# Modulations 3 to 5 in feed-forward groups 1 to 3, the mix norm's first tile in the last group, three buffers in the decay block

## The reference

```
mods = (silu(c) @ w_ada + b_ada)                     # 9 vectors of 1024 for each of 9 sequences
sh1, sc1, gt1, sh2, sc2, gt2, sh3, sc3, gt3 = mods
x = x + 0.5 * gt1 * swiglu(rms_norm(x, g1) * (1 + sc1) + sh1)      # first feed-forward
P = (rms_norm(x, g2) * (1 + sc2) + sh2) @ w_in                      # input projection, 2560 columns
#   columns 0..1791 -> RWKV-7 heads, 1792..2559 -> sliding-window attention
#   decay d = exp(-exp(w_log)), w_log and a from two 64-wide products; keys normed; running products of d
x = x + gt2 * concat(rwkv7(P), attention(P)) @ w_out
x = x + 0.5 * gt3 * swiglu(rms_norm(x, g3) * (1 + sc3) + sh3)      # second feed-forward
y = rms_norm(x, g_final)
```

## Time and profile before

| | |
|---|---|
| median of 3 runs | 2608.36 us (2606.34 to 2609.14) |
| profiled execution, its own time | 2612.36 us |
| its span | 2610.6 us |
| PE busy | 2461.0 us, 94% of the span, 22194 matmuls |
| DVE / ACT / POOL busy | 1134.9 / 389.7 / 495.5 us |
| mean granted TensorE clock | 0.96 |

### The profile page before, as it was taken

How to read it: one execution, slowest core, us unless ns; L and a number is a source line. 1 busy time by engine, 2 the same in 40 slices (tenths; PEclk the granted TensorE clock), 3 DMA queues, 4 the chain that set the end, 5 groups by cost and what they waited for, 6 DMA issues and landing times. The chain is left out here.

```text
span 2610.6 us, 51884 instructions
## 1 busy us (share of the span) xinstructions
PE 2461.0 (94%) x22194; PEld 2331.8 (89%) x22194; DVE 1134.9 (43%) x2521; ACT 389.7 (15%) x894; POOL 495.5 (19%) x233
## 2 busy tenths in 40 slices
PE   5999999999999699998689999988999999999996
PEld 4999999999998598886279996888999999999995
DVE  4533344434441554343566654217444344433335
ACT  4100000000000324343511113113000000000003
POOL 3322122112210221110500004314221222122110
PEclk8999999999999799998699999898999999999997
DMA  8211111111113331011510001212101111111102
GB/s 319 81 49 32 48 48 30 34 48 48 48 32 129 102 99 37 25 33 47 203 46 4 4 4 61 80 30 81 49 18 47 48 48 48 48 48 42 38 0 76
DMA packets 157638, 151.14 MB, mean 58 GB/s; under 512 B 21441, under 2 KB 138866, under 8 KB 156969
## 3 DMA queue, kind: packets, MB, share of 16 engines
q1 hardware_dynamic: 156824, 142.29, 17.3%
q0 software_dynamic: 528, 4.53, 0.4%
q10 hardware_dynamic: 144, 2.23, 0.2%
HBM read 137.98 MB, written 11.34 MB: 57 GB/s over the span
## 5 line engine op out<-in xcount | busy, mean ns | idle before, releaser
L474 PE MATMUL bank<-hh,f_up_hi 128*128 128x364 f32 (+1 forms) x2112 | 697.0, 330 | 11.8 <-ACT hh L414 9.4
L475 PE MATMUL bank<-hl,f_up_hi 128*128 128x364 f32 (+1 forms) x2112 | 696.0, 330 | 0.0
L476 PE MATMUL bank<-hh,f_up_lo 128*128 128x364 f32 (+1 forms) x2112 | 695.7, 329 | 0.0
L474 PEld LDWEIGHTS bank<-hh,f_up_hi 128*128 128x128 f32 x2112 | 398.8, 189 | 14.8 <-issue 14.8
L872 DVE TENSOR_TENSOR f_prod<-f_silu,bank 128x364 f32<-128x364 f32 x132 | 70.2, 532 | 780.9 <-PE bank L476 780.9
L475 PEld LDWEIGHTS bank<-hl,f_up_hi 128*128 128x128 f32 x2112 | 398.8, 189 | 0.0
L476 PEld LDWEIGHTS bank<-hh,f_up_lo 128*128 128x128 f32 x2112 | 398.8, 189 | 0.0
L489 DVE SCALAR_TENSOR_TENSOR x<-bank,mods,x 128x364 f32<-128x364 f32 (+2 forms) x552 | 310.7, 572 | 200.4 <-PE bank L476 185.1
L725 POOL TENSOR_TENSOR f_up_lo<-f_up_raw,f_up_hi 128x2048 fp32r<-128x2048 f32 x44 | 202.9, 4610 | 803.1 <-DVE f_up_hi L859 803.1
L474 PE MATMUL bank<-f_a_hi,f_dn_hi 128*128 128x364 f32 (+1 forms) x1056 | 347.0, 329 | 0.6 <-issue 0.6
L476 PE MATMUL bank<-f_a_hi,f_dn_lo 128*128 128x364 f32 (+1 forms) x1056 | 346.9, 328 | 0.0
(11 more groups left out here) (348 smaller groups left out, 2855.4 us busy)
## 6 DMA issues: line engine op xcount, KB each, us to landing
f_up_raw<-in_ffn_w_gu SPq DMA_DIRECT2D x88, 512.0 KB, 4.9
f_dn_raw<-in_ffn_w_down SPq DMA_DIRECT2D x22, 1024.0 KB, 7.7
gates<-in_w_ada SPq DMA_DIRECT2D x16, 1024.0 KB, 4.8
ada<-in_w_ada SPq DMA_DIRECT2D x12, 1024.0 KB, 15.9
late<-in_w_ada SPq DMA_DIRECT2D x8, 1024.0 KB, 5.2
w_in_raw<-in_w_in SPq DMA_DIRECT2D x16, 512.0 KB
x_spill<-x POOLq DMA_DIRECT2D x1, 4352.0 KB, 15.1
x_in<-in_x_prompt SPq DMA_DIRECT2D x8, 512.0 KB, 8.3
```

The lines of the kernel that those rows point to most:

```text
L474: pe.matmul(out, wh, rh, start=(n == 0), stop=False)
L475: pe.matmul(out, wh, rl, start=False, stop=False)
L476: ins = pe.matmul(out, wl, rh, start=False, stop=(n == last))
```

## The change

Three parts. (1) Modulations 3, 4 and 5 are made in feed-forward groups 1, 2 and 3, one in each group, which become a loop of their own; the four loads of a modulation go one after another through the raw buffer of the down weights, which stands empty then. Modulation 4 is finished (`finish_mods`) at the start of the last group's down sums. (2) The last group no longer holds modulation products. It holds the loads of the first two `w_in` chunks, the split of the first, the write of x to DRAM tile by tile (now SP's queue), means of the mix norm for tiles 0 and 1, and the whole scaling of tile 0, whose 8 steps on DVE stand one behind each down sum of the third tile. The projection block begins with the split of chunk 1 and tiles 1 and 2 of the norm; PE starts with product (0,0). Chunk 0 of `w_in` has a third pair of split buffers. (3) The decay block makes only modulations 6 to 8; its small weights and the first modulation load are issued at the end of the projection block; three buffers take the place of two.

```diff
...
 
+    def step(self, dve, t, c):
+        k, (a, n), v = self.k, self.spans(t), KD * t + c
+        if c == 0:
+            dve.wait_ge(self.spread_mm, t + 1)
+        if v >= 4:
+            if c % 2:
+                dve.wait_ge(self.lo_odd, (v - 3) // 2)
+            else:
+                dve.drain()
+        dve.scalar_tensor_tensor(self.t[c % 4][:, 0:n], k.x[:, c, a:a + n], k.mod(self.i_shift + 1, c),
+                                 self.bank[t][:, 0:n], ALU.mult, ALU.mult).then_inc(self.t_done, 1)
+        if c % 2 == 1 and c >= 3:
+            self.low(dve, t, c - 3, self.lo_even)
+        if c == KD - 1:
+            self.low(dve, t, KD - 2, self.lo_even)
...
     if first:
-        ada = Ada(k, "ada", (0, 1, 2), [HH_AT + 8 * KB * s for s in range(8)] + [WT_AT + KB * a for a in (24, 32, 40, 48)], 7, [(7, 256)])
-        late = Ada(k, "late", (3, 4), [WT_AT, WT_AT + 40 * KB], 7, [(7, 256), (0, 0)])
+        ada = Ada(k, "ada", [HH_AT + 8 * KB * s for s in range(8)] + [WT_AT + KB * a for a in (24, 32, 40, 48)], 7)
+        late = Ada(k, "late", [WT_AT + 40 * KB], 7)
...
+        mix = k.mix = Norm(k, "mix", 3, 0, WT_AT + 8 * KB, WT_AT + 20 * KB, WT_AT + 28 * KB)
+        x_final, k.spilled = k.sem("x_final"), k.sem("x_spilled")
+    LATE = range(1, 4) if first else range(1, 1)
...
+            if first:
+                with sp.Fori(LATE.start, LATE.stop) as g:
+                    next_up(g, 0)
+                    sp.wait_ge(dn_lo_done, g + 1)
+                    for q in range(4):
+                        if q == 3:
+                            next_up(g, 1)
+                        if q:
+                            sp.wait_ge(late.used, 4 * g + q)
+                        late.load(sp, g + 2, q, 0)
+                    sp.wait_ge(late.used, 4 * g + 4)
+                    load_dn(g + 1)
...
             if first:
                 sp.wait_ge(up_lo_done, FC * NGRP)
-                sp.wait_ge(dn_lo_done, NGRP)
-                for s in range(8):
-                    late.load(sp, s)
+                win.load(sp, 0, win.first[0])
+                win.load(sp, 1, win.first[1])
+                for t, (a, n) in enumerate(TILES):
+                    sp.wait_ge(x_final, 2 * t + 2)
+                    sp.dma_start(k.dram["x_spill"][:, :, a:a + n], k.x[:, :, a:a + n]).then_inc(k.spilled, 16)
...
+            if first:
+                win.low(pool, 0)
+                mix.odd_lows(pool, 0)
...
                     pe.wait_ge(up_lo_done, FC * g + j + 1)
                     for t in range(NT):
+                        u = NT * j + t
                         up(g, j, t)
-                pe.wait_ge(dn_lo_done, g + 1)
-                for t in range(NT):
-                    down(g, t)
+                        if modulation and 1 <= u <= 4:
+                            if u == 1:
+                                pe.wait_ge(dn_free, ND * g + 4)
+                            late.product(pe, u - 1, 0, 4 * g + u - 4)
+                if modulation:
+                    late.turn(pe, g - 1, late_turned)
+                downs(g)
+                if modulation:
+                    pe.wait_ge(late.added, g)
 
             def first_group():
...
-                        if u in (0, 1, 4, 5):
-                            s = {0: 0, 1: 2, 4: 4, 5: 6}[u]
-                            late.product(pe, s)
-                            late.product(pe, s + 1)
-                        if u == 3:
-                            late.turn(pe, 0)
                 pe.wait_ge(dn_lo_done, g + 1)
-                pe.wait_ge(late.rows, 2)
                 for t in range(NT):
-                    down(g, t)
-                    if t == 0:
-                        late.turn(pe, 1)
+                    for c in range(KD):
+                        down(g, t, c)
+                        if t >= 1 and c == 3:
+                            mix.means(pe, t - 1)
+                        if t == 1 and c == KD - 1:
+                            mix.spread(pe, 0)
 
...
+            if first:
+                with pe.Fori(LATE.start, LATE.stop) as g:
+                    group(g, True)
+            with pe.Fori(LATE.stop, NGRP - (1 if first else 0)) as g:
...
+            if first:
+                for j in range(2):
+                    mix.squares(act, 0, j, x_final)
+                mix.roots(act, 0)
+                for j in range(2):
+                    mix.squares(act, 1, j, x_final)
+                mix.highs(act, 0, True)
 
...
 
-            def group(g):
+            def group(g, modulation=False):
                 for u in range(NU):
                     gated(g, u)
                     if u % NT == NT - 1:
                         j = u // NT
                         up_head(j, FC * g + FC + j + 1, NU * g + NT * (j + 1))
+                    if modulation and u == 4:
+                        late.copy(dve, g)
+                if modulation:
+                    late.add(dve, g - 1, g + 2, late_turned)
                 for v in range(ND):
...
-                        late.add(dve, 0)
-                    if first and u == 5:
-                        late.copy(dve, 1)
+                if not first:
+                    for v in range(ND):
+                        summed(g, v)
+                    return
+                dve.wait_ge(dn_lo_done, NGRP)
+                win.high(dve, 0)
+                finish_mods(dve, k, 4)
                 for v in range(ND):
+                    t, c = v // KD, v % KD
                     summed(g, v)
-                    if first and v == KD:
-                        late.add(dve, 1)
+                    if c in (3, KD - 1):
+                        dve.drain().then_inc(x_final, 1)
+                    if t == 1 and c == 6:
+                        mix.inverse(dve, 0)
+                    if t == 2:
+                        mix.step(dve, 0, c)
+                mix.inverse(dve, 1)
 
...
+class InWeights:
...
+        self.first = [k.at(f"w_in_first{j}", WT_AT + 4 * KB * j, [P, KD, P]) for j in range(2)]
+        self.raw = [k.at(f"w_in_raw{j}", R2_AT + 4 * KB * j, [P, KD, P]) for j in range(2)]
+        hi = [k.at(f"w_in_hi{j}", at, [P, KD, P], F32R) for j, at in enumerate((GATE_AT, GATE_AT + 8 * KB, WT_AT + 40 * KB))]
+        lo = [k.at(f"w_in_lo{j}", at, [P, KD, P], F32R) for j, at in enumerate((GATE_AT + 4 * KB, GATE_AT + 12 * KB, WT_AT + 44 * KB))]
...
+            win.load(sp, 3, win.raw[1])
             norm.ready(sp, NT - 1)
-            sp.wait_ge(spilled, 16)
+            sp.wait_ge(k.spilled, 16 * NT)
+            sp.wait_ge(lo_done, 2)
             sp.dma_start(cos[:], d["cos"]).then_inc(tab_in, 16)
...
+            sp.wait_ge(lo_done, NC)
+            sp.dma_start(k.w2a2[0:HD, :], d["rwkv_w2"][0]).then_inc(k.lora_in, 16)
+            sp.dma_start(k.w2a2[HD:P, :], d["rwkv_a2"][0]).then_inc(k.lora_in, 16)
+            sp.dma_start(k.keep[:], d["scan_keep"]).then_inc(k.keep_in, 16)
+            sp.wait_ge(mm_done, at(NC - 2, NT - 1))
+            k.gates.load(sp, 6, 0, 0)
...
 
             for t in range(NT):
                 norm.ready(pe, t)
+                if t == 1:
+                    norm.spread(pe, 2)
                 for n in range(2):
                     if t == 0:
                         pe.wait_ge(lo_done, n + 1)
                     product(n, t)
+                    if t == 0 and n == 0:
+                        norm.spread(pe, 1)
+                        norm.means(pe, 2)
                 if t == 0:
-                    norm.spread(pe, 2)
+                    previous()
             for n in range(2, NC):
                 pe.wait_ge(lo_done, n + 1)
...
-            for s in range(16):
-                ada.load(sp, s)
+            for s in range(1, 12):
+                if s >= 3:
+                    sp.wait_ge(ada.used, s - 2)
+                ada.load(sp, 6 + s // 4, s % 4, s % 3)
             sp.wait_ge(k.shift_out, 32)
...
                 if 1 <= i < PAIRS:
                     back(i)
-                if i in (4, 8, 11):
-                    for q in range(4):
-                        ada.product(pe, 4 * (4, 8, 11).index(i) + q)
-                if i in (5, 9):
-                    ada.turn(pe, (i - 5) // 4)
+                if i == 5:
+                    ada.turn(pe, 0, turned)
+                if i in (4, 8):
+                    modulation(i // 4 - 1)
+            ada.turn(pe, 1, turned)
+            modulation(2)
             pe.wait_ge(rates_done, 2 * NU)
             pe.wait_ge(rk_done, 1)
             for i in range(NU):
                 bonus(i)
-                if i == 1:
-                    ada.turn(pe, 2)
                 if i == 5:
-                    for s in range(12, 16):
-                        ada.product(pe, s)
-                if i == 9:
-                    ada.turn(pe, 3)
+                    ada.turn(pe, 2, turned)
...
+            def modulation(n):
+                ada.add(dve, n, 6 + n, turned)
+                if n:
```

(6 more changed lines are left out.)

318 lines of the change are left out of this document (159 added, 159 removed).

## The result

| | before | changed | ratio, 95% interval |
|---|---|---|---|
| first comparison, 4 runs each | 2608.1 us | 2582.7 us (2581.2 to 2587.3) | 0.9906 [0.9889, 0.9924] |
| a second, later, 7 and 4 runs | 2609.9 us | 2580.8 us (2579.0 to 2583.3) | 0.9888 [0.9872, 0.9905] |

The account below looks back on a forecast made before the run. PE was taken as the bound, so time counts only where it waits, runs at low clock or loses work. Gains of 4.1 + 16.7 + 14.0 = 34.8 us gave 2577.6 profiled, 2573.5 for the median; range 2562 to 2586.

Parts of the forecast that it names:

- a pair took 1.93 us, one is 0.97 ... and I allow 0.5: Feed-forward groups 1 to 3: four added modulation products cost 3.9 us plus 0.5 for turns, 4.4 a group, 13.2 in all.
- DVE's tail: End of the last group: DVE's third-tile sums and norm steps end about 16.6 us after PE starts that tile's down sums.
- Both reasons go: Projection block's start: DVE's 16.11 us wait for w_in goes, since loads are issued a group earlier and the spill is split.
- product (0,0) 4.0, plus 2.0 ...; spread 0.8; then tile 1's scaling: Projection block's start: first product, low-clock extra and spread precede DVE's 8.4 us scaling, within 35.2 us to the third weight.
- The wait of 3.08 for w2a goes: Decay block's start: PE's 3.08 us wait for w2a vanishes, so everything up to lora 4 is 3.1 us earlier.
- the forecast's middle: Middle of the decay block: products 4 to 7 end about 1267, third tile's sigmoids begin about 1271.3 instead of 1275.71.
- The term behind the first bonus, 4.6: Decay block's end: first bonus to next block takes 5.0 to 5.5 us instead of 10.4, a gain of 4.6.
- the fourth is issued only after product 8 has run: Third modulation of the decay block: fourth load issued at 1278.7, first bonus at 1285.3 against 1294.68, 9.4 us gained.
- (a): Rival: exclusive DVE/POOL port lock in the last group's tail and beside tile 1 holds DVE 3.9 us and more; 2579; chance 0.14.
- (b): Rival: ACT, DVE and POOL, not loads, pace the decay block's middle; 7 us less gain, 2580.5; chance 0.12.
- (c): Rival: in groups 1 to 3 the single buffer makes twelve products wait 7 us and more, above 2650; chance 0.03.
- (d): Rival: the gap only moves, PE's wait for the norm appears in full in the last group; 2585 to 2590; chance 0.04.

Follow-up runs that it names:

- the second profiles: Repeat profiles of the unchanged kernel before (2610.4 us) and of the changed kernel with nothing altered (median 2580.8 us).
- the norm's own experiment: Changed kernel with the mix norm wholly in the projection block again, early input-weight loads and spill by tiles kept: 2584.2 us, ratio 0.9896.

## Why the prediction was right, and where not

**Direction and shape were right, the size was read too large**: every stretch gained where it was said to. The median came out at 2582.7 us where 2573.5 was forecast. That is inside the stated range but above the forecast's own 2566 to 2581: the range holds because it was widened for the rivals and the bounds of the parts. Of the 9.2 us missed, 4.0 are the difference between profile and median that was carried over unchanged (the changed kernel's profile lies at its median), 6.3 are the three parts together, and 1.2 the other way were gained outside them, where nothing was forecast. Of the marks it set, it met: PE without a wait in groups 1 to 3, the first product 17 us after the first third-tile sum (862.72 to 879.45: 16.7), first bonus at 59 us (59.4), waits for gates 6 to 8 us (7.7), decay block under 85 (82.3). Missed by little: groups of 76.2 us (76.9), PE standing 6 to 7 us at the end of the last group (8.25), the last group at 82 to 84 us (84.8 with that stand). Not met: PE's waits at tile 1 and at the third tile, forecast as 2 to 3 and 2 us, both for DVE; they were 3.63, released by POOL's low part, and 0.60.

**Part 1, forecast 4.1, measured 2.3.** The step that failed is "a pair took 1.93 us, one is 0.97 ... and I allow 0.5". The pair's second half ran behind a product, the new ones stand alone between up units, and each costs 1.20 with its two seams; 4.4 us a group were reckoned. Taking them out gave 15.0 us back, 5.0 a group. That the loads are hidden held.

**Part 2, forecast 16.7, measured 13.3.** Reckoned from S (861.7): first product at S + 17.8 against 17.4, behind it 37.2 against 35.2, and 1.1 more ahead of S. The terms of DVE's tail were near: a sum with its step 1.40 us where 1.52 was reckoned. Behind the start the terms were, as measured and as reckoned: first product 6.5 and 6.0, spread of tile 1 until DVE starts 1.1 and 0.8, tile 1's scaling with its tail 9.2 and 9.3, spread and third tile 12.3 and 11.1, two products 8.1 and 8.0. The step mis-sized most is the spread of the third tile: PE had stood 3.6 us from 892.6, its clock was low again until 901.8, and DVE's start came 2.09 us after this spread's, where it was 1.14 for tile 1. No term held that. The slow products beside it cost nothing, since PE still waits 0.60 for DVE behind them. Near in its terms, the part was wrong in its account. "Both reasons go" is true of the weights' wait: with the early loads and the spill by tiles, without the early norm, the gain is 12.6. But the norm ahead of the block, on which most of my arithmetic went, gave 0.6 or nothing, because the step "product (0,0) 4.0, plus 2.0 ...; spread 0.8; then tile 1's scaling" was taken over as it stood in the code and not asked whether it need be so. In it DVE, the engine I had named as late next, waits 7.2 us for a spread queued behind a product that nobody needs yet. Moving it, with the sums and the spread of tile 2, gave 6.7.

**Part 3, forecast 14.0, measured 12.9** (and 13.0 between the second profiles, 90.5 and 77.5). "The wait of 3.08 for w2a goes" was mis-sized: it is 1.6 to 1.8 in two other profiles. And the forecast's middle, in which PE's products pace the block, is refuted: with the loads gone waits for ACT take their place (4.1 to 13.0 us). The term behind the first bonus, 4.6, does not follow from its own row: 10.4 less 5.0 to 5.5 is 4.9 to 5.4. It measured 4.1, and 6.5 between the second profiles. What saved the number is that the forecast itself took lora 5 to 7 out of PE's hands (it named ACT and DVE, the traces show ACT and POOL), and that the term that counts was put right: "the fourth is issued only after product 8 has run".

**The rivals.** (a) The port lock in full did not come. In the last group DVE's lows and POOL's subtracts alternate and never meet. Behind it they do; DVE's and POOL's timelines there:

```profile
893.35 0.95 POOL L407 TENSOR_TENSOR hl<-mix_t,hh 128x364 fp32r<-128x364 f32 x1 [1.53 <-ACT mix_t L417]
893.77 1.44 DVE L399 SCALAR_TENSOR_TENSOR hl<-mix_t,mods,hh 128x364 fp32r<-128x364 f32 x2
901.71 0.82 POOL L407 TENSOR_TENSOR hl<-mix_t,hh 128x296 fp32r<-128x296 f32 x1 [0.23 <-ACT mix_t L417]
901.96 0.90 DVE L399 SCALAR_TENSOR_TENSOR hl<-mix_t,mods,hh 128x296 fp32r<-128x296 f32 x1
```

Two lows take 1.44 us where two alone took 1.10, one takes 0.90 where another took 0.52: 0.7 us in all. Twice DVE's low starts first and POOL's subtract is the longer one, 1.33 us at 889.38 and 1.07 at 900.41 where it takes 0.95 and 0.82. That is the direction of the rule that the prediction cites from the Trainium skill (SBUF — State Buffer, "SBUF: two separate sides"), at less than the price of the rival, since the two engines seldom met. (b) is true of the middle, as the experiments without loads and with two buffers show, but its price of 7 us did not come: the gains ahead of the middle and behind it stayed. (c) did not come; landings in the single buffer were 4.8 to 5.8 us. (d) forecast 2585 to 2590 for a gap that only moves. Its time did not come, but its thought, that the early norm buys nothing and the end of the wait for the loads all, is nearer to what the norm's own experiment showed than my account was.

## What to carry to other kernels

Ask of each moved piece what it is worth alone, with the other pieces in place: gains measured one at a time need not add, since two edits may cure the same wait or both hold a third piece (here the spill by tiles), and the larger gain may lie with the smaller edit. When the forecast names the engine that is late next, look through the queues of the engines that feed it for anything that stands ahead of its operand. And reckon an inserted piece with both its seams, from a row where it stands alone.

## What the runs showed of the hardware

- The granted clock was 0.50 of full for 5.3 us after PE had stood 8.3 us, and for some 5.5 us more after it had stood 3.6 us. With 40 matmuls in the first of these stands it stayed at 1.00, across a turn of blocks of 1.6 us without work. In another execution of the same order (without loads in the decay block) the clock was back 3.0 us after PE's start and the first product took 5.4 us instead of 6.5: the level comes back at different times, and the two executions where it came early there have the stretch of 119 us instead of 121. With the norm in the projection block the clock fell to 0.50 for 3.4 us after PE had stood only 2.3.
- The sixteen matmuls of 256 columns of one modulation product took 1.07 us where the granted clock was 1.00 and 1.94 where it was 0.50. In the decay block they came at either level after a wait for a load: 1.94 after 2.4 and 3.5 us in the changed kernel, 1.07 after 3.3 with the small loads back and after 4.0 before.
- A DVE cast of 128x1024 took 0.69 us alone and 1.63 beside POOL's subtract of the same size (2.04 in the earlier trace rows).
- Identical code behind the changed parts, 1290 us long, scattered by 5 us between executions (1289.0 to 1294.0).
